# The shift's product with the first block's columns moves from TensorE to VectorE

## The reference

```python
def modulate(h, shift, scale):
    return h * (1 + scale[:, None, :]) + shift[:, None, :]

mod = jax.nn.silu(c) @ w_ada[l] + b_ada[l]
sh_m, sc_m, gt_m, sh_f, sc_f, gt_f = jnp.split(mod, N_MOD, axis=-1)
h = modulate(rms_norm(x, g_mix[l]), sh_m, sc_m)
y = token_mixer(h, w_in[l], ...)            # begins with h @ w_in
x = x + gt_m[:, None, :] * y
h = modulate(rms_norm(x, g_ffn[l]), sh_f, sc_f)
x = x + gt_f[:, None, :] * swiglu(h, w_gate[l], w_up[l], w_down[l])
```

## Time and profile before

| | |
|---|---|
| median of three runs | 2037.68 us (2037.05 to 2037.9) |
| the profiled execution's own time | 2036.13 us |
| its span, first to last instruction | 2034.3 us |
| TensorE busy | 2028.0 us, 100% of the span |
| VectorE busy | 1220.3 us, 60% |
| ScalarE busy | 897.1 us, 44% |
| GpSimd busy | 1040.5 us, 51% |
| granted TensorE clock | 1.000 of full speed, the mean of the core |

### The profile page before, as it was taken

How to read it: one execution, slowest core, us unless ns; L and a number is a source line. 1 busy time by engine, 2 the same in 40 slices (tenths; PEclk the granted TensorE clock), 3 DMA queues, 4 the chain that set the end, 5 groups by cost and what they waited for, 6 DMA issues and landing times.

```text
span 2034.3 us, 29907 instructions
## 1 busy us (share of the span) xinstructions
PE 2028.0 (100%) x10916; PEld 1713.7 (84%) x10916; DVE 1220.3 (60%) x2154; ACT 897.1 (44%) x1367; POOL 1040.5 (51%) x773
## 2 busy tenths in 40 slices
PE   9999999999999999999999999999999999999999
PEld 7788778889889878877788899898877788989898
DVE  5677335576757637854356767567445478647363
ACT  5124353536446422244445355364446544536352
POOL 5454334476565754443355755556343334556555
PEclk9999999999999999999999999999999999999999
DMA  6322213343543343321233444423221213233333
GB/s 222 107 104 83 83 63 101 117 164 107 187 145 125 104 130 101 104 83 65 81 113 125 141 150 145 166 104 104 88 94 64 82 42 103 85 104 105 104 104 104
DMA packets 37492, 223.99 MB, mean 110 GB/s; under 512 B 6012, under 2 KB 6524, under 8 KB 11744
## 3 DMA queue, kind: packets, MB, share of 16 engines
q1 hardware_dynamic: 31424, 193.48, 27.6%
q10 hardware_dynamic: 5920, 28.55, 4.1%
HBM read 215.59 MB, written 2.10 MB: 107 GB/s over the span
## 4 chain that ended last, share of the span: by engine, by line
PE 98%; DVE 1%; DVEq 0%; issue 0%; ACT 0%; ACTq 0%
PE ps L599 18%; PE ps L601 18%; PE ps L600 18%; PE ps L751 6%; PE ps L753 6%; PE ps L752 6%; PE ps L616 4%; PE ps L617 4%; PE ps L618 4%; PE ps L679 2%; PE ps L648 1%; PE ps L650 1%; PE ps L649 1%; PE ps L700 1%; PE ps L689 1%; PE ps L721 0%
## 5 line engine op out<-in xcount | busy, mean ns | idle before, releaser
L519 POOL TENSOR_TENSOR w_lo<-w_raw,w_hi 128x512 fp32r<-128x512 f32 x544 | 733.1, 1378 | 775.4 <-ACT w_hi L1165 765.0
L1165 ACT ACTIVATE w_hi<-w_raw 128x2048 fp32r<-128x2048 f32 x134 | 256.1, 1911 | 384.1 <-PE ps L601 282.4
L599 PE MATMUL ps<-a_hi,w_hi 128*128 128x512 f32 (+1 forms) x888 | 351.9, 396 | 0.0
L601 PE MATMUL ps<-a_hi,w_lo 128*128 128x512 f32 (+1 forms) x888 | 346.3, 390 | 0.0
L600 PE MATMUL ps<-a_lo,w_hi 128*128 128x512 f32 (+1 forms) x888 | 345.8, 389 | 0.0
L533 POOL TENSOR_TENSOR w_lo<-w_raw,w_hi 128x512 fp32r<-128x512 f32 x164 | 215.0, 1333 | 159.4 <-ACT w_hi L1292 159.4
L601 PE MATMUL ps<-b_hi,w_lo 128*128 128x512 f32 x612 | 238.1, 389 | 0.0
L599 PE MATMUL ps<-b_hi,w_hi 128*128 128x512 f32 x612 | 238.1, 389 | 0.0
L600 PE MATMUL ps<-b_lo,w_hi 128*128 128x512 f32 x612 | 238.1, 389 | 0.0
L599 PEld LDWEIGHTS ps<-a_hi,w_hi 128*128 128x128 f32 (+1 forms) x888 | 165.3, 186 | 47.5 <-issue 9.2
L601 PEld LDWEIGHTS ps<-a_hi,w_lo 128*128 128x128 f32 (+1 forms) x888 | 165.3, 186 | 37.0
(11 more groups left out here) (391 smaller groups left out, 4529.2 us busy)
## 6 DMA issues: line engine op xcount, KB each, us to landing
w_raw<-in_weights SPq DMA_DIRECT2D x176, 1024.0 KB, 4.9
v<-in_ada ACTq DMA_DIRECT2D x24, 1024.0 KB, 4.9
out<-x SPq DMA_DIRECT2D x8, 256.0 KB, 2.0
x<-in_x_in SPq DMA_DIRECT2D x3, 512.0 KB, 7.5
w_raw<-in_weights SPq DMA_DIRECT2D x4, 256.0 KB, 6.0
yc<-in_c_rows ACTq DMA_DIRECT2D x2, 512.0 KB, 3.2
bias<-in_mult_bias ACTq DMA_DIRECT2D x1, 640.0 KB
x<-in_x_in SPq DMA_DIRECT2D x2, 256.0 KB, 4.7
```

The lines of the kernel that those rows point to most:

```text
L519: nc.gpsimd.tensor_tensor(w_lo[:, s, piece], w_raw[:, s, piece], f32(w_hi[:, s, piece]), ALU.subtract).then_inc(w_lo_ready, 1)
L599: nc.tensor.matmul(o, wh, hi(kt), start=kt == 0, stop=False)
L601: last = nc.tensor.matmul(o, wl, hi(kt), start=False, stop=kt == depth - 1)
L1165: nc.scalar.activation(w_hi[:, n % 2, :], w_raw[:, n % 2, :], ACT.Copy).then_inc(w_hi_ready, 1)
```

## The change

`shift_rows`, `shift_turn`, `shift_low`, the two ScalarE instructions that make the high part of the shift, and the two that copy the rows out go away, with `shift_parts` and four semaphores. In their place VectorE multiplies the 256 columns of each of the eight row tiles of the raw weights (`w_raw`) with that tile's shift (a number for each partition) and adds them up in `shift_acc`, 128x256 of the tile `yc`. At e = 0 four of the eight stand ahead of the wait for the sums and four behind the two spreads; at e = 1 all eight stand where `shift_low(1)` stood. TensorE then adds over the partitions with the same two products with ones that it had in `shift_turn`, now over 128 partitions instead of 2. Since VectorE reads `w_raw`, SyncE waits for `shift_summed` before it overwrites the slots of these two blocks (block 126 over 124, block 145 over 143).

```diff
+SHIFTED_BLOCKS = [LAYERS * LAYER_BLOCKS, LAYERS * LAYER_BLOCKS + C_FF]
...
-        shift_row = g[0:2, 2, 0:2 * P]
+        shift_acc = yc[:, 5, 0:2 * P]
...
+                if n - 2 in SHIFTED_BLOCKS:
+                    sync.wait_ge(shift_summed, SHIFTED_BLOCKS.index(n - 2) + 1)
                 sync.dma_start(w_raw[:, n % 2, :], weights[n]).then_inc(w_loaded[n % 2], 16)
...
-            def shift_rows(s, e):
-
-                pe.wait_ge(shift_split, e + 1)
-                for kt in range(KT):
-                    for w in (w_hi, w_lo):
-                        last = nc.tensor.matmul(ps[7][0:2, 0:2 * P], shift_parts[:, kt, :], wcols(w, s, KT, kt, 0, 2 * P),
-                                                start=kt == 0 and w is w_hi, stop=kt == KT - 1 and w is w_lo)
-                last.then_inc(shift_done, 1)
-
-            def shift_turn(e):
-
-                pe.wait_ge(shift_copied, e + 1)
+            def shift_column(e):
+
+                pe.wait_ge(shift_summed, e + 1)
                 for u in range(2):
-                    last = nc.tensor.matmul(ps[7][:, 2 * u:2 * u + 2], shift_row[:, u * P:(u + 1) * P], ones[0:2, 0:2],
+                    last = nc.tensor.matmul(ps[7][:, 2 * u:2 * u + 2], shift_acc[:, u * P:(u + 1) * P], ones[:, 0:2],
                                             start=True, stop=True)
                 last.then_inc(shift_turned, 1)
...
                     if kt == 3 + e:
-                        shift_turn(e)
+                        shift_column(e)
...
-                    if kt == KT - 1:
-                        shift_rows(s, 0)
...
-                shift_rows(s, 1)
...
-            nc.scalar.activation(shift_parts[:, :, 0], mod[:, 0:KT], ACT.Copy).then_inc(shift_hi, 1)
...
-                    if n == (5, 3)[e]:
-                        act.wait_ge(shift_done, e + 1)
-                        nc.scalar.activation(shift_row, ps[7][0:2, 0:2 * P], ACT.Copy).then_inc(shift_copied, 1)
...
+            def shift_products(e, tiles):
+
+                block_ = (0, C_FF)[e]
+                if tiles.start == 0:
+                    dve.wait_ge(w_loaded[block_ % 2], nth(L, LAYER_BLOCKS // 2, block_ // 2, 16))
+                for kt in range(KT)[tiles]:
+                    w, of = wcols(w_raw, block_ % 2, KT, kt, 0, 2 * P), mod[:, 3 * KT * e + kt:3 * KT * e + kt + 1]
+                    if kt == 0:
+                        last = nc.vector.tensor_scalar(shift_acc, w, of, None, ALU.mult)
+                    else:
+                        dve.drain()
+                        last = nc.vector.scalar_tensor_tensor(shift_acc, w, of, shift_acc, ALU.mult, ALU.add)
+                if tiles.stop == KT:
+                    last.then_inc(shift_summed, 1)
+
             mean, root_, inverse = (qcol[:, e, 0:2 * TT] for e in range(3))
+            shift_products(0, slice(0, HK))
             dve.wait_ge(ss_done, nth(L, 2, 0))
...
-            shift_low(0)
+            shift_products(0, slice(HK, KT))
             dve.wait_ge(rms_turned, nth(L, 2, 0))
...
-            shift_low(1)
+            shift_products(1, slice(0, KT))
             for n in range(KT):
```

More of the change, by code:

```diff
@@ L235, in two_blocks @@
         next_gain = sb("next_gain", [P, KT])
-        shift_parts = sb("shift_parts", [P, KT, 2], F32R)
         shift_sum = sb("shift_sum", [P, 2])
@@ L311, in two_blocks @@
         xm_split = sem("xm_split")
-        shift_hi = sem("shift_hi")
-        shift_split = sem("shift_split")
-        shift_done = sem("shift_done")
         plain_used = sem("plain_used")
         plain_scaled = sem("plain_scaled")
-        shift_copied = sem("shift_copied")
+        shift_summed = sem("shift_summed")
         shift_turned = sem("shift_turned")
@@ L1493, in modulated @@
                     act.wait_ge(xm_ready, base + n + 1)
-                    e = base // KT
-                    if n == (5, 3)[e]:
-                        act.wait_ge(shift_done, e + 1)
-                        nc.scalar.activation(shift_row, ps[7][0:2, 0:2 * P], ACT.Copy).then_inc(shift_copied, 1)
                     if base == 0 and n < KT - 1:
@@ L1639, in _ @@
                     w_split(L, C_OUT + 3)
-            nc.scalar.activation(shift_parts[:, :, 0], mod[:, 3 * KT:4 * KT], ACT.Copy).then_inc(shift_hi, 1)
             for n in range(KT):
@@ L2203, in _ @@
                                       inverse[:, c:c + TT].unsqueeze(2).to_broadcast([P, TT, P])).then_inc(spread, 1)
[L2204 to L2208, removed]
             def shift_taken(e):
```

## The result

| | before | after |
|---|---|---|
| median of 12 runs each | 2037.13 us (2035.82 to 2037.9) | 2041.88 us (2040.5 to 2042.49) |
| the profiled execution's own time | 2036.13 us | 2041.87 us |
| its span | 2034.3 us | 2040.1 us |
| TensorE busy | 2028.0 us | 2027.1 us |
| VectorE busy | 1220.3 us | 1230.4 us |

A forecast was written before the change was run, and what follows sets the result against it. TensorE, 98% of the chain of waits, was taken to bound the kernel. First entry 2.2 plus second entry 2.7 made 4.9 us slower: 2041.0 against the profiled execution, 2042.6 against the median; range 2037.7 to 2043.8 us.

The forecast's parts named there:

- What bounds the kernel: Chain of waits is 98% TensorE: work leaving it counts fully unless it then waits; waits it suffers are lost.
- The cost of one new instruction: On VectorE: 1.44 us while GpSimd has pieces left, 0.56 us after that; the first, a multiplication alone, nearest 348 ns.
- First entry: At e = 0: `modulated` 3.9 us late, less 1.84 us slack at the first square, 2.05 us slower; taken as 2.2.
- the allowance for GpSimd starting first: First entry: if GpSimd is first at 1413.19, up to 0.5 us more, so 2.2 taken instead of 2.05.
- my two ends: First entry: the spreads start 1.0 to 1.37 us after the reciprocal, making them 1.9 to 2.25 us late.
- Second entry: At e = 1: first addition to `x` 2.85 us late, 0.15 us given back by removed rows, so 2.7 us slower.
- What the removed products give back: Sixteen TensorE products per entry, 3.74 us together at most; nothing at the first entry, some 0.15 us at the second.
- Edits at nothing: Costed at nothing: SyncE's wait holding block 126, with 6 us of cover, and products with ones over 128 partitions.
- No hold-up: Rival: GpSimd does not hold up the new VectorE instructions, each 0.56 us; no change, 2037.8 us; chance 0.12.
- one place only: Rival: only one entry is held up, 2.2 or 2.7 us slower, 2039.9 to 2040.4 us; chance 0.13.
- the rows come out: Rival: removed rows leave TensorE's time and nothing waits; 3.74 us faster, 2033.9 us; chance 0.03.
- The pauses cost more than their length: Rival: TensorE's new pauses drop its clock to the lower level, 2 us more, 2044.6 us; chance 0.06.

The follow-up runs named there:

- psum_late: Kernel before with the new way at the first entry only, running sum in PSUM, all eight instructions behind the spreads; 2038.93 us, ratio 1.001.
- psum_acc: Changed kernel with the running sum in PSUM bank 7, only the last of the eight instructions writing `shift_acc`; 2036.5 us, ratio 1.0002 to the kernel before.
- rows_kept: Changed kernel with sixteen dead TensorE products at each entry in place of the removed ones; 2041.79 us, ratio 1.0025 to the kernel before.
- no_product: Changed kernel without the shift's product: no sum on either engine, the two products with ones read constants; 2035.93 us, ratio 0.9994 to the kernel before.
- e0_only: Kernel before with the new code at the first entry only; 2039.05 us, ratio 1.0011.
- e1_only: Kernel before with the new code at the second entry only; 2039.93 us, ratio 1.0015.
- the first comparison: Twelve runs each of the kernel before and the changed kernel; medians 2037.13 and 2041.88 us, ratio 1.0023.
- upper-group: The slower of two groups of a kernel's executions by time; for the kernel before 2036.95 us and above, against 2035.4 to 2036.6 in the lower.
- split7: Changed kernel with the running sum in PSUM and, at the first entry, seven instructions ahead of the mean, one behind the spreads; 2037.06 us, ratio 1.0.
- filler_sized: Changed kernel with 3, 7 and 5 dead products in TensorE's first-entry pauses (ahead of sums, spreads, first modulated tile); 2041.68 us, ratio 1.0021 to the kernel before.
- before_filler3: Kernel before with three dead products (six instructions) in TensorE's pause ahead of the first entry's sums; 2036.09 us, ratio 0.9995.
- before_filler: Kernel before with seven dead products (fourteen instructions) in TensorE's pause ahead of the first entry's sums; 2036.47 us, ratio 0.9999.
- split7_filler: As split7, with three dead products in bank 4 ahead of the first entry's sums; 2035.99 us, ratio 0.9997 to the kernel before.

## Why the prediction was right, and which term was off

- *What bounds the kernel.* Right. VectorE's lateness came out on TensorE one for one once the slack was used (`psum_late`: 3.81 late, 2.02 lost).
- *The cost of one new instruction.* Right: 0.54 us with its drain where GpSimd is idle (2.18 / 4), 1.42 beside GpSimd's pieces (4.26 / 3; 1.44 forecast). `psum_acc` shows the cause.
- *First entry, the term that was mis-sized.* Forecast 2.2 (2.05 without the allowance for GpSimd starting first), measured 1.70. VectorE got to its new work earlier than I had it and was the first at the ports, so the allowance of 0.15 was not needed. Behind the mean the spreads came 1.0 us after the reciprocal (1418.43 to 1419.42), the lower of my two ends. `modulated` was 3.4 us late, not 3.9; less the 1.84 of slack that is 1.57. The squares' products start 1.35 + 0.25 = 1.60 us late, and the second product behind them 1.70.
- *Second entry.* Forecast 2.7, measured 2.68; but its parts differ a little. Three held-up instructions were forecast and three found (1.21 and, by the 5.58 us of all seven, two of the seven). The first addition to `x` came 1672.79 - 1667.05 - 3.02 = 2.72 us late, not 2.85, and the removed products gave back nearly nothing of it, not 0.15. The pause at the fifth tile was 1.48 us by its row, not 1.8; behind it TensorE was held by the modulated tile and by the next block's low piece, as the last rows had it.
- *What the removed products give back.* Right that waits swallow it: `rows_kept` costs no more than the changed kernel, and `no_product` gains 1.0 to 2.1 us and not 3.74. At the second entry the forecast put the part kept at 0.15; no run measured it alone, and the changed profile leaves 0.04 (2.72 - 2.68).
- *Edits at nothing.* No row shows a wait for block 126, and TensorE waits nowhere for the shift's sum; both hold.
- *The rivals.* "No hold-up" falls with the 4.26 us, "one place only" with `e0_only` and `e1_only`, "the rows come out" with `no_product`. "The pauses cost more than their length" is half right: the clock did fall in the profiled execution, for 1.57 us. But it also falls in the kernel before, in about half of its executions, and both sides of the first comparison had nine of twelve such runs. So it explains the 5.74 us between the profiled pair and no part of the 4.75 between the medians. The forecast's 4.9 was added to a median that was an upper-group one, which came out right because the changed kernel's is one too; that was luck. So is part of the closeness of 4.9 to 4.75: the rows give 4.38.

Whether the new pauses make the fall more likely stays open. By time, the upper group holds 9 of 12 executions of the changed kernel, 9 of 11 of `e0_only`, 8 of 11 of `e1_only` and 8 of 10 of `rows_kept`, but only 4 of 11 of `psum_acc` and 6 of 11 of `split7`, whose sum lies in PSUM; before has 53 of 104, and 9 of 12 in the first comparison. By a mean clock under 1.000 the same six have 11 of 12, 10 of 11, 8 of 11, 10 of 10, 7 of 11 and 8 of 11, against 44 of 92 in before. The second count hints that they do, but the first comparison has no clocks of before to set beside it, and no run changes the pauses alone.

## What to carry to other kernels

Before work is moved from the engine that bounds to one that idles, see what runs beside its new place: a VectorE instruction with two SBUF inputs beside GpSimd cost 1.42 us instead of 0.54, and putting one operand in PSUM took that away without moving anything. Removed work is worth only what the next wait lets through; leave it out altogether once (`no_product`) and you have the ceiling, here 1 to 2 us of 3.74, before any replacement is tuned. And before two profiled executions are subtracted, look at their granted clocks: 1.57 us of 5.74 were not the change's.

## What the runs showed of the hardware that was not expected

TensorE's clock fell to 0.50 in the changed kernel, which keeps it busy all but 13 of 2040 us, and in the variants. The falls seen came behind a pause of 0.1 to 0.7 us followed by sixteen products of one or two columns: at 1413.7 to 1415.4 behind the sums (`e1_only`, `no_product`, `psum_late`, `split7`), near 1440 behind the squares (the changed kernel, `e0_only`, `rows_kept`, `filler_sized`, and a second fall in `psum_late` and `split7`). They lasted 3.4 us, twice 6.8 us (`no_product`, `psum_late`); the changed kernel's took in eight products and cost 1.57 us. The same code in another execution kept 1.00. With six dead instructions of 128 columns in the pause ahead of the sums all 11 executions of `before_filler3` stayed at 1.000, and with fourteen all 11 of `before_filler`, where 53 of 104 of the unchanged kernel lie in the upper group. The Trainium skill ("TensorE: Matmul & The Clock Gate", section "What's actually happening") has the chip watch TensorE's activity without regard to where the kernel starts, so that one kernel may fare differently from run to run; the two groups agree with that. Where the fall lies in an upper-group execution of the kernel before was not seen in a profile. The fillers that cure it point to the sums' pause, and so do `e1_only`, `no_product` and `psum_late`: up to there their TensorE runs the same instructions as before, and the clock fell there.

Even tiny VectorE instructions wait: the one of 128x4 from SBUF to SBUF (L2195, in the other kernels L2198, L2238, L2239 or L2244) took 0.37 to 1.15 us beside a GpSimd piece, and one of the same size that reads PSUM (L2190) 0.15 beside the same pieces. In `split7_filler` that was 1.0 us more, about as much as two of the large ones with GpSimd idle (2 x 0.54).
